# Up projection of a gated FFN by seven block products: ten of eleven column pairs in place of eight

## The reference

```python
def swiglu(h, w_gate, w_up, w_down):
    return (jax.nn.silu(h @ w_gate) * (h @ w_up)) @ w_down

x = x + mix @ w_out[l]
x = x + swiglu(rmsnorm(x, norm2_g[l]), w_gate[l], w_up[l], w_down[l])
return rmsnorm(x, norm_f_g)
```

## Time and profile before

| | |
|---|---|
| median of three runs | 770.68 us |
| the profiled execution, its own time | 770.01 us |
| its span, first to last instruction | 768.3 us |
| DVE busy | 435.5 us, 57% |
| ACT busy | 276.2 us, 36% |
| weight loads (q1) | 74.5 MB, 30% of the DMA engines' time |
| the FFN's pairs 1 to 10 on PE | 431.1 to 642.5 us |

### The profile page before, as it was taken

The page is one execution under the profiler, slowest core; times in us unless marked ns, Lnnn a source line. Parts: engine busy times, 40 slices in busy tenths (PEclk is TensorE's granted clock), DMA queues, the critical chain, the costliest instruction groups (busy, mean ns, idle before and its releaser), DMA issues.

```text
span 768.3 us, 10404 instructions
## 1 busy us (share of the span) xinstructions
PE 759.5 (99%) x4215; PEld 639.6 (83%) x4215; DVE 435.5 (57%) x653; ACT 276.2 (36%) x451; POOL 24.1 (3%) x51
## 2 busy tenths in 40 slices
PE   9999999999999999999999999999999999999996
PEld 7988888888676788888889889999999988888885
DVE  5878635257978524344257766666666677313123
ACT  6444122344555332232244333233333354313111
POOL 5000000012100000000000000000000000000000
PEclk9999999999999999999999999999999999999999
DMA  8423323301111134233313313332233243322302
GB/s 248 144 104 110 110 94 125 109 1 56 56 56 57 56 120 170 94 110 96 123 56 110 110 55 111 110 107 78 90 110 91 79 161 110 109 82 83 110 1 109
DMA packets 61796, 75.16 MB, mean 98 GB/s; under 512 B 3682, under 2 KB 49842, under 8 KB 61748
## 3 DMA queue, kind: packets, MB, share of 16 engines
q1 hardware_dynamic: 61744, 74.50, 30.0%
q10 hardware_dynamic: 4, 0.00, 0.0%
HBM read 72.40 MB, written 2.10 MB: 97 GB/s over the span
## 4 chain that ended last, share of the span: by engine, by line
PE 72%; issue 1%; DVE 0%; ACT 0%; POOLq 0%; POOL 0%; ACTq 0%
PE bank L1404 23%; PE bank L1405 23%; PE bank L1406 22%; PE bank L1667 1%; PE bank L1629 1%; PE bank L1650 1%; PE bank L1636 0%; PE bank L1417 0%; PE bank L1633 0%; DVE w_lo L861 0%; ACT square_out L532 0%; ACT x L823 0%; DVE x L1376 0%; DVE work L1027 0%; POOLq L163 0%
## 5 line engine op out<-in xcount | busy, mean ns | idle before, releaser
L861 DVE TENSOR_TENSOR w_lo<-stage,w_hi 128x1024 fp32r<-128x1024 f32 (+1 forms) x125 | 148.1, 1188 | 177.6 <-ACT w_hi L555 168.8
L1404 PE MATMUL bank<-hT_hi,w_hi 128*128 128x512 f32 (+1 forms) x648 | 236.3, 365 | 0.6 <-DVE hT_lo L846 0.6
L1405 PE MATMUL bank<-hT_lo,w_hi 128*128 128x512 f32 (+1 forms) x648 | 233.6, 361 | 0.0
L1406 PE MATMUL bank<-hT_hi,w_lo 128*128 128x512 f32 (+1 forms) x648 | 233.6, 361 | 0.0
L555 ACT ACTIVATE w_hi<-stage 128x1024 fp32r<-128x1024 f32 x126 | 129.4, 1029 | 170.7 <-PE bank L1406 169.6
L1404 PEld LDWEIGHTS bank<-hT_hi,w_hi 128*128 128x128 f32 x648 | 122.4, 189 | 18.9 <-POOL w_lo L496 0.8
L1406 PEld LDWEIGHTS bank<-hT_hi,w_lo 128*128 128x128 f32 x648 | 122.3, 189 | 18.6
L1405 PEld LDWEIGHTS bank<-hT_lo,w_hi 128*128 128x128 f32 x648 | 122.5, 189 | 17.5
L1404 PE MATMUL bank<-w_hi,aT_hi 128*128 128x512 f32 x176 | 68.5, 389 | 0.0
L1405 PE MATMUL bank<-w_lo,aT_hi 128*128 128x512 f32 x176 | 68.5, 389 | 0.0
L1406 PE MATMUL bank<-w_hi,aT_lo 128*128 128x512 f32 x176 | 68.5, 389 | 0.0
(11 more groups left out here) (214 smaller groups left out, 995.0 us busy)
## 6 DMA issues: line engine op xcount, KB each, us to landing
stage<-in_w_in SPq DMA_DIRECT2D x21, 1024.0 KB, 5.3
stage<-in_w_gate SPq DMA_DIRECT2D x11, 1024.0 KB, 5.3
stage<-in_w_up SPq DMA_DIRECT2D x11, 1024.0 KB, 5.3
stage<-in_w_down SPq DMA_DIRECT2D x22, 512.0 KB, 4.3
stage<-in_w_out SPq DMA_DIRECT2D x4, 1024.0 KB, 4.9
x_nat<-in_x SPq DMA_DIRECT2D x4, 512.0 KB, 5.5
stage<-in_w_br_mlstm SPq DMA_DIRECT2D x4, 512.0 KB, 3.5
stage<-in_w_br_fox SPq DMA_DIRECT2D x4, 512.0 KB, 4.5
```

The source lines that it names most:

```text
L861: dve.tensor_tensor(ring_part(w_lo, g), staged(g), ring_part(w_hi, g).bitcast(F32), ALU.subtract).then_inc(lo_split, 1)
L1404: pe.matmul(o, a_hi, b_hi, start=first, stop=False)
L1405: pe.matmul(o, a_hi, b_lo, start=False, stop=False)
L1406: return pe.matmul(o, a_lo, b_hi, start=False, stop=last)
```

## The change

SEVEN goes from pairs 2 to 9 to pairs 1 to 10. Functions are made general for a gate run of seven (SEVEN_GATE), but that set is empty. So that pair 1 can be in the set:

- the eight steps of token_sums are put in pair 0 and the first half of pair 1, t_sum moves to other memory, and PE asks for three t_lo at the second granule of the first run and for the fourth at its last product;
- the sums of weights for a run are made right after the low split of the run's first granule, three granules ahead, and no longer at the start of the pair.

Pair 10's run is the last work ahead of the down projection. Only aT 0 to 3 are split within it, and the other 18 in the down stage (SPLIT_F from 12 to 4), for which ACT first waits until PE has used every granule of the FFN and DVE has made the last sum of products. PE claims the run's banks one by one, and not all at the start. The down stage's code on PE is unchanged.

```diff
-SEVEN = range(2, 10)
-SPLIT_F = 12
+SEVEN = range(1, 11)
+SEVEN_GATE = ()
+LAST_PLAIN = F_BLOCKS
+SPLIT_F = 4
+UP_RUN = (3, 2, 6, 7)
+GATE_RUN = (1, 0, 4, 5)
-T_STEPS_AT = {(0, 0): (0, 1), (0, 1): (2,), (0, 2): (3,), (0, 3): (4,), (1, 0): (5,), (1, 1): (6,), (1, 2): (7,)}
-T_HI_AT = {(0, 2): (2, 3), (1, 0): (0, 5), (1, 1): (1, 6), (1, 2): (3, 8)}
-T_LO_AT = {(0, 3): (2, 1), (1, 0): (0, 2), (1, 1): (1, 3), (1, 3): (3, 4)}
+T_STEPS_AT = {(0, 0): (0, 1), (0, 1): (2, 3), (0, 2): (4,), (0, 3): (5,), (1, 0): (6,), (1, 1): (7,)}
+T_HI_AT = {(0, 1): (2, 3), (0, 2): (0, 5), (0, 3): (1, 6)}
+T_LO_AT = {(0, 3): ((0, 2), (2, 1)), (1, 0): ((1, 3),)}
...
+            def next_lo(g):
+                split_lo(ffn_ahead(g))
+                if ffn_ahead(g) in runs:
+                    weight_sums(ffn_ahead(g))
...
 # DVE, a pair with a run
+                g = ffn_up[p]
+                if p in SEVEN:
+                    if p not in SEVEN_GATE:
+                        gated(p, 0)
+                        gated(p, 1)
+                    next_lo(g)
+                    next_lo(g + 1)
+                    if p == SEVEN[0]:
+                        take_t_lo(3, 4)
+                    run_sums(g, 0)
+                    run_sums(g, 1)
+                    if last:
+                        take_aT_lo(0)
+                        take_aT_lo(1)
+                    next_lo(g + 2)
+                    run_sums(g, 2)
+                    run_sums(g, 3)
+                    if last:
+                        take_aT_lo(2)
+                        take_aT_lo(3)
+                    run_sums(g, 4)
+                    times_quarters(p, runs.index(g))
+                    next_lo(g + 3)
...
 # ACT, a pair with a run
+                if p in SEVEN:
+                    split_hi(ffn_ahead(g))
+                    if p in SEVEN_GATE:
+                        ffn_tanh_pair(p)
+                    if p == SEVEN[0]:
+                        take_t_hi(3, 8)
+                    keep_first(g)
+                    for n in range(1, 4):
+                        split_hi(ffn_ahead(g + n))
+                        if p == F_BLOCKS // 2 - 1 and n < 3:
+                            act.wait_ge(used, g + n + 1)
+                            for m in range(2):
+                                take_aT_hi(2 * (n - 1) + m)
...
+            act.wait_ge(used, G_DOWN)
+            act.wait_ge(up_step, UP_STEPS * len(runs))
             for n in range(2 * D_GRAN - RING):
...
 # PE, a run of seven
-                take(6, (up_step, UP_STEPS * i + 4))
-                take(7, (up_step, UP_STEPS * i + 5))
                 pe.wait_ge(lo_split, g + 1)
-                seventh(3, low_t, g, 0, *h[0, 0])
-                seventh(2, low_t, g, half, *h[1, 0], used)
+                seventh(one, low_t, g, 0, *h[0, 0])
+                seventh(two, low_t, g, half, *h[1, 0], used)
                 pe.wait_ge(lo_split, g + 2)
                 if i == 0:
+                    pe.wait_ge(t_lo_ready, 3)
+                take(five, (up_step, UP_STEPS * i + 4))
+                seventh(two, high_t, g + 1, 0, *t[1])
+                seventh(five, low_t, g + 1, half, *t[0], used)
+                pe.wait_ge(lo_split, g + 3)
+                take(last, (up_step, UP_STEPS * i + 5))
+                seventh(five, high_t, g + 2, 0, *t[2])
+                seventh(last, low_t, g + 2, half, *h[1, 1], used)
+                pe.wait_ge(lo_split, g + 4)
+                if i == 0:
                     pe.wait_ge(t_lo_ready, 4)
+                seventh(last, high_t, g + 3, half, *t[3], used)
```

More of the change, by code:

```diff
@@ L137, in block_kernel, with seven_slot @@
     G_FFN = len(granules)
-    ffn_first, combos = [], {}
+    ffn_first, ffn_up, combos, runs = [], [], {}, []
+    def seven_slot(w, col):
+        g = len(granules)
+        combos[g + 1], combos[g + 2] = (len(runs), 0), (len(runs), 1)
+        runs.append(g)
+        src = w[:, col:col + 2 * P].rearrange("(k p) c -> p k c", p=P)
+        slot([lambda st: whole(KD)(st)[:, :, 0:P], None, None, lambda st: whole(KD)(st)[:, KD // 2:, P:2 * P]],
+             [(whole(KD), src)])
     for i in range(F_BLOCKS // 2):
         ffn_first.append(len(granules))
[L141 to L150, removed]
+        (seven_slot if i in SEVEN_GATE else column_slot)(w_g, 2 * P * i)
+        ffn_up.append(len(granules))
+        (seven_slot if i in SEVEN else column_slot)(w_u, 2 * P * i)
     G_DOWN = len(granules)
@@ L767, in ffn_tanh_of, with ffn_tanh_pair, keep_first @@
                     act.wait_ge(mix_lo_ready, 8)
-                act.activation(work[n][:, :], psum[4 * (p % 2) + n][:, :], ACT.Tanh, scale=0.5).then_inc(ffn_tanh, 1)
+                act.activation(tanh_pair[:, n, :], psum[4 * (p % 2) + n][:, :], ACT.Tanh, scale=0.5).then_inc(ffn_tanh, 1)
+            def ffn_tanh_pair(p):
+                act.wait_ge(up_step, UP_STEPS * (runs.index(ffn_first[p]) + 1))
+                act.wait_ge(ffn_step, 4 * (p - 1) + 2)
+                act.activation(tanh_pair[:, :, :], gate_quarters[:, :, :].rearrange("p (j n) t -> p j (n t)", j=2), ACT.Tanh,
+                               scale=0.5).then_inc(ffn_tanh, 2)
+            def keep_first(g):
+                i = runs.index(g)
+                act.wait_ge(used, g + 1)
+                if i >= 1:
+                    act.wait_ge(up_step, UP_STEPS * i)
+                act.activation(parts[:, 0, :], psum[1 if g in ffn_first else 3][:, low_t], ACT.Copy).then_inc(kept, 1)
             def take_t_hi(m, n_steps):
@@ L798, in _ @@
                         split_hi(ffn_ahead(g + n))
                 else:
-                    for n in range(2, 4):
+                    for n in range(2):
                         split_hi(ffn_ahead(g + n))
-                        if p == F_BLOCKS // 2 - 1:
+                        if p == LAST_PLAIN:
+                            act.wait_ge(used, g)
                             for m in range(3):
                                 take_aT_hi(3 * n + m)
+                        ffn_tanh_of(p, n)
@@ L1258, in times_up, with run_sums @@
                                          op1=ALU.mult).then_inc(ffn_step, 1)
[L1260 to L1264, removed]
-                             (parts[:, 2:4, :], bank5, parts[:, 1:2, :].to_broadcast([P, 2, SEQ // 2])),
-                             (quarters[:, 3, :], psum[6][:, low_t], parts[:, 3, :]),
-                             (quarters[:, 1:3, :], bank7, parts[:, 2:4, :]))[step]
+            def run_sums(g, step):
+                i = runs.index(g)
+                banks, whole_of = (GATE_RUN, gate_quarters) if g in ffn_first else (UP_RUN, quarters)
+                bank2, bank5, bank7 = (psum[b][:, :].rearrange("p (n t) -> p n t", n=2) for b in banks[1:])
+                out, a, b = ((whole_of[:, 0, :], bank2[:, 0, :], parts[:, 0, :]),
+                             (parts[:, 1, :], bank2[:, 1, :], parts[:, 0, :]),
+                             (parts[:, 2:4, :], bank5, parts[:, 1:2, :].to_broadcast([P, 2, SEQ // 2])),
+                             (whole_of[:, 3, :], bank5[:, 0, :], parts[:, 3, :]),
+                             (whole_of[:, 1:3, :], bank7, parts[:, 2:4, :]))[step]
+                if step == 0:
+                    dve.wait_ge(used, g + 2)
+                    dve.wait_ge(kept, i + 1)
+                    if i and g not in ffn_first:
+                        dve.wait_ge(ffn_step, 4 * ffn_up.index(g))
                 if step in (2, 3):
                     dve.wait_ge(up_step, UP_STEPS * i + step)
+                if step == 2:
+                    dve.wait_ge(used, g + 3)
+                if step == 4:
+                    dve.wait_ge(used, g + 4)
                 dve.tensor_tensor(out, a, b, ALU.add).then_inc(up_step, 1)
@@ L1320, in take_aT_lo @@
                                   ALU.subtract).then_inc(aT_lo_ready, 1)
+            def next_lo(g):
+                split_lo(ffn_ahead(g))
+                if ffn_ahead(g) in runs:
+                    weight_sums(ffn_ahead(g))
             for p in range(F_BLOCKS // 2):
+                last = p == F_BLOCKS // 2 - 1
                 g = ffn_first[p]
[L1324 to L1344, removed]
-                else:
[L1346 to L1351, removed]
+                if p in SEVEN_GATE:
+                    next_lo(g)
[7 more added lines that the diff above has]
+                    next_lo(g + 3)
+                    gated_pair(p)
+                else:
+                    for n in range(2):
+                        next_lo(g + n)
+                        if p == LAST_PLAIN:
                             for m in range(3):
@@ L1780, in up_in_seven @@
                 half = KD // 2
-                take(3, (kept, i + 1))
-                take(2, (up_step, UP_STEPS * i + 2))
-                take(6, (up_step, UP_STEPS * i + 4))
-                take(7, (up_step, UP_STEPS * i + 5))
+                one, two, five, last = GATE_RUN if g in ffn_first else UP_RUN
+                take(one, (kept, i + 1))
```

(19 more changed lines are left out.)

77 lines of the change are left out of this document (61 added, 16 removed).

## The result

The changed kernel takes 773.03 us, median of 11 runs, against 770.53 us for the kernel before, median of 11: a ratio of 1.0026, 95% interval 1.0018 to 1.0034. It is slower by 0.26% (the medians are 2.5 us apart; the ratio, which compares the means, gives 2.0), where I forecast +0.65 us and no change. Its 11 times stand on two levels: four from 771.23 to 771.75 (mean 771.4), seven from 772.80 to 773.37 (mean 773.1). All 11 count as undisturbed. The kernel before has one level, 770.03 to 770.98.

A forecast was written before the change was run, and what follows sets the result against it. PE was taken as the bound, its pitches making up the time. Two shorter pairs (-1.6 us) and a wait at the down projection (+2.25) gave +0.65 us, 771.3 from a median of 770.68, no change; range 769.6 to 772.7.

The forecast's parts named there:

- The pitches: Pairs 1 and 10 on PE: with a run of seven they take 20.95 and 20.98 us, 1.6 us less together.
- Edits at nothing, and pairs 0 and 1: Pairs 0 to 9: earlier weight sums and token sums cost PE nothing; thinnest cover 0.6 us, at pair 1's last product.
- the third rival: Pair 1's last product, 450.66: DVE is late with t_lo3; beyond 0.6 us of slip each us costs one; chance 0.12.
- The passage: From pair 10 to the down projection: claiming all four banks makes PE wait 2.25 us for DVE's fifth sum of products.
- PE starts 0.15 after that: Start of the down stage: PE resumes 0.15 us after DVE's fifth sum ends, as at 11.38 after 11.23.
- PE's clock falls after the new gap: Down stage behind the gap: one granule at 1.2 GHz costs 5.44 us more, 776.7 us; chance 0.04.
- a clock under 9 tenths after 640 us: Sign on the changed profile, from the down stage on, that would show PE's clock falling after the gap.
- The numbers: Whole kernel: 0.83 for within 0.2%, 0.07 for faster, 0.10 for slower, of which clock 0.04, late pair 1 0.04, noise 0.02.
- The shorter wait: Passage to the down projection: PE waits only 1.0 to 1.5 us, time 770.1 us; chance 0.12.
- No wait at all: Passage to the down projection: it is covered and all 1.6 us are kept, time 769.1 us; chance 0.06.
- The shorter pitch: Runs of seven on PE: by the skill's rule two pairs save 2.4 us, time 770.5 us; chance 0.02.

The follow-up runs named there:

- experiment 1: Changed kernel, but the down stage claims each of its four banks just before its first product in it: 768.95 us, against 770.56 for the kernel before.
- experiment 5: Changed kernel with runs of seven in pairs 1 to 9 only, pair 10 plain and splitting 12 blocks of aT: 769.91 us, against 770.66 for the kernel before.
- experiment 3: Changed kernel with the last run's fifth sum put ahead of the low halves of aT 2 and 3 on DVE, to shorten PE's wait: 770.46 us.
- experiment 4: Changed kernel with one more DVE operation, its result unused, ahead of the last run's fifth sum, to lengthen PE's wait: 774.27 us.
- experiment 6: Changed kernel with runs of seven in pairs 2 to 10 only, pair 1 plain: 772.57 us.
- experiment 7: Kernel before, with PE also made to wait at the down stage's start for the low half of the third down granule: 773.41 us.

## Why the prediction was right, and where it was not

**The pitches.** Right. Pair 1 measured 20.95, the two pairs together 770.56 - 768.95 = 1.6 us (experiment 1), one of them 0.75 (experiment 5, forecast 0.81).

**Edits at nothing, and pairs 0 and 1.** Right. t_lo3 was forecast to run from 448.7 to 449.9, with pair 1 starting at 431.14. In the changed kernel pair 1 starts 0.39 later, and the row stands 0.36 later:

```profile
449.06 1.22 DVE L1348 TENSOR_TENSOR t_lo<-t_sum,t_hi 128x1024 fp32r<-128x1024 f32 x1
```

PE waited for nothing there; the third rival did not occur. ACT's split that I let wait for pair 2's up weights until 452.3 started at 452.62.

**The passage.** Right in place, cause and order; the size of the wait was 0.2 us short. The term "PE starts 0.15 after that" measured 0.39. The nearest row, 11.38, is a wait for one operand ahead of a 256-column product near the start of the kernel. That wait took 0.15 in the changed kernel as well (11.61 to 11.76), so the row was read rightly, but the restart at the passage is slower; why is not shown. At the passage PE resumed 0.39 us after the release, and in experiments 3, 4, 6 and 7 after 0.40, 0.39, 0.37 and 0.36. The forecast's 2.25 us thus became 2.49.

**The clock.** Here the prediction failed. I gave "PE's clock falls after the new gap" a chance of 0.04; by the times it happened in 7 of 11 executions, and so in the median. The sum without it, 771.3 us, is close to the changed kernel's lower level (771.4). Part of that closeness is luck: the wait was 0.24 us longer than the sum had it, and the median of before came out 0.15 lower than the 770.68 that it started from. I had two rows for gaps, of 1.1 and 0.6 us, called them PE's longest idle times, and took them as evidence for one of 2.25 us. Both the reading and the use were wrong. The 1.1 us lie ahead of the kernel's first matmul, so that they are no gap between matmuls. The longest such wait is one of 0.67 us at 188 us, which I had passed over:

```profile
1.05 1.23 PE L1492 MATMUL bank<-ones 128*128 128x128 f32 x4 [1.05 <-POOL ones L439]
...
188.57 1.16 PE L1603 MATMUL bank<-v_m,decay 128*128 128x129 f32 x8 [0.67 <-DVE work L1089]
```

A wait of 0.67 us says nothing about one more than three times as long. The price was off as well: 5.44 us for a whole down granule at 1.2 GHz, where the stretch lasted 3.4 us and cost 1.7; with that price the rival's time would have been 773.0, which is the median measured. And the sign that I had named for this rival, a clock under 9 tenths after 640 us, does not show on the page: 3.4 us at half speed leave 0.91 of a slice of 19.3 us. What leant on the Trainium skill ("TensorE: Matmul & The Clock Gate", section "HAM oscillation — how this bites in real kernels") leant wrong: it warns of idle gaps longer than these, and the runs show falls at gaps of 2.4 to 2.5 us, in some executions and not in others. The measurement decides. At the passage, experiment 3's gap of 1.3 us without a fall agrees with it, and so does experiment 4's of 3.6 with one; the fall behind 1.8 us at the start of experiment 3's trace does not.

**The numbers.** The stated range ended at 772.7; the ratio put on the median it was made from, 770.68 x 1.0026, gives 772.7, and the median of the 11 runs, 773.03, lies 0.3 above it. The chance of slower by over 0.2%, 0.10, was too small, above all by the clock's 0.04.

**The other rivals.** The shorter wait did not come by itself; experiment 3 made it, 770.46 against 770.1 worked out, and most of the difference is again the later restart (0.25). No wait at all was excluded by the queue order, and came with experiment 1: 768.95 against 769.1. The shorter pitch is out: 256-column matmuls start 0.12 us apart in the changed kernel too.

What stays open: what decides, execution by execution, whether a gap of 2.4 to 2.5 us makes the clock fall. The shares differ between kernels with the same gap (2 of 10 and 7 of 11), and the number of runs is too small to say whether the kernel or chance makes that difference. The chip may have a part in it as well: experiments 1 to 4 ran on one chip, 6 and 7 on another. Why the fall of experiment 4 comes within the gap, and that of the changed kernel 1.0 us behind it, is not shown either.

## What to carry to other kernels

When a stage claims several banks, make each claim where its bank is first written: here two moved lines turned a loss of 2.5 us into a gain of 1.6 us. When the last step of a loop is changed, check what its successor asks first; a wait that no other iteration has can hide behind it. And when PE is the bound, a new gap is to be priced twice, once for its length and once for the slow matmuls that may follow, unless several executions with a gap of the same length show that they don't. One profile is not enough: experiment 6 has the gap of 2.5 us with a full clock.

## What the runs showed of the hardware

- In the profiled execution of the changed kernel the granted clock fell 1.0 us after PE had resumed from a gap of 2.5 us, to its lower level for 3.4 us. With a gap of 3.6 us (experiment 4) it fell within the gap, and PE resumed at half speed and kept it for 5.4 us.
- Behind a wait of 1.81 us near the start of experiment 3's trace the clock was at its lower level for 3.4 us as well.
- The same program with the same gap has times on two levels, 1.7 us apart (773.1 and 771.4), and 1.7 us is what the fall costs in the profiled one. A median of few runs can fall on either.
- With ten dummy products in the gap all 11 times stayed below the upper level, and the clock of the profiled execution was full.
- PE resumed 0.36 to 0.40 us after the end of the DVE operation that it waited for, in five kernels, ahead of a 512-column product; 0.15 us ahead of a 256-column one at the start of the kernel, before and after the earlier trace rows.
